# Streaming conv/gated-DeltaNet/PEER layer on one core: a third expert of four is multiplied in rounded pieces, and GpSimd subtracts the first table's remainders

## The reference, cut to what matters

```python
q = (x2 @ w_q).reshape(n, PEER_HEADS, 2, PEER_HALF)
s = jnp.einsum('nhpd,hpkd->nhpk', q, sub_keys)      # top 16 per half, then top 16 of the 256 sums
...
hid = jnp.einsum('pd,phkd->phk', xb, u[ib])         # first table, rows u
act = jax.nn.gelu(hid) * gb                         # gb: softmax gates of the 128 chosen experts
return jnp.einsum('phk,phkd->pd', act, v[ib])       # second table, rows v
```

## Time and profile before

| | |
|---|---|
| median of 3 runs | 4827.29 us (4825.91 to 4842.75) |
| the profiled execution, its own time | 4846.23 us |
| its span | 4844.7 us |
| TensorE busy | 4618.2 us, 95% |
| VectorE, ScalarE, GpSimd busy | 3317.9, 1250.0, 1277.3 us (68%, 26%, 26%) |
| DMA busy from 3,600 us on | 0.97 of 16 engines |

### The profile page before, as it was taken

One profiled execution on the slowest core, in us unless ns is written; L12 is line 12 of the kernel. 1 busy time (PEld: TensorE's weight loads), 2 busy tenths in 40 slices (PEclk: granted clock), 3 DMA queues, 4 the chain that ended last, 5 costly groups with the idle time before them and its releaser, 6 DMA issues. The chain is left out here.

```text
span 4844.7 us, 82402 instructions
## 1 busy us (share of the span) xinstructions
PE 4618.2 (95%) x27693; PEld 4287.9 (89%) x27693; DVE 3317.9 (68%) x4283; ACT 1250.0 (26%) x1766; POOL 1277.3 (26%) x936
## 2 busy tenths in 40 slices
PE   8999989999998999999679999999999999999995
PEld 8999989999997999999668888888888888888884
DVE  4889873343433330168887888888888888888887
ACT  4232323222222221232462222222222222222221
POOL 0111132221122332233002333333333333332332
PEclk8999999999999999999899999999999999999997
DMA  3222223221234342221378999999999999999998
GB/s 117 85 89 85 87 66 97 71 74 55 71 95 158 122 158 89 96 97 60 105 227 336 361 351 365 366 362 368 368 362 369 364 372 362 366 366 367 365 360 326
DMA packets 283622, 1084.63 MB, mean 224 GB/s; under 512 B 23696, under 2 KB 104464, under 8 KB 209936
## 3 DMA queue, kind: packets, MB, share of 16 engines
q0 software_dynamic: 74752, 538.99, 28.8%
q1 hardware_dynamic: 168336, 400.91, 25.1%
q10 hardware_dynamic: 40320, 142.10, 7.6%
HBM read 1017.03 MB, written 64.88 MB: 223 GB/s over the span
## 5 line engine op out<-in xcount | busy, mean ns | idle before, releaser
L486 PE MATMUL ps<-xhi,hi 128*128 128x320 f32 x2560 | 773.5, 315 | 31.2 <-POOL lo L1388 15.8
L486 PE MATMUL ps<-xlo,hi 128*128 128x320 f32 x2560 | 761.7, 311 | 0.0
L2479 PE MATMUL ps<-aT,work 128*128 128x384 f32 x2048 | 750.1, 489 | 4.1 <-DMA work<-in_v_units 4.1
L2445 PE MATMUL ps<-xhi,whi 128*128 128x384 f32 x2048 | 692.1, 338 | 0.0
L2445 PE MATMUL ps<-xlo,whi 128*128 128x384 f32 x2048 | 686.4, 335 | 0.0
L2797 DVE CUSTOM_DVE_ANT_0 work<-work,keep 128x2048 f32<-128x2048 f32 x256 | 585.1, 2286 | 33.4 <-DMA work<-in_peer_u,cur_u 22.1
L2762 DVE SCALAR_TENSOR_TENSOR keep<-work,act_w,keep 128x2048 f32<-128x2048 f32 x256 | 600.5, 2346 | 7.3 <-DMA work<-in_peer_v,cur_v 5.9
L2487 PE MATMUL ps<-ahi,vhi 128*128 128x384 f32 x1024 | 495.1, 484 | 32.2 <-DVE vlo L2735 32.0
L486 PEld LDWEIGHTS ps<-xhi,hi 128*128 128x128 f32 x2560 | 484.8, 189 | 36.3 <-POOL lo L1388 16.3
L2860 POOL DMA_INDIRECT work<-in_peer_v,cur_v x256 | 306.3, 1196 | 797.7 <-DVE keep L2762 770.5
L2479 PEld LDWEIGHTS ps<-aT,work 128*128 128x128 f32 x2048 | 381.6, 190 | 142.7 <-issue 7.7
(11 more groups left out here) (334 smaller groups left out, 7760.5 us busy)
## 6 DMA issues: line engine op xcount, KB each, us to landing
work<-in_v_units ACTq DMA_DIRECT2D x256, 512.0 KB, 8.0
work<-in_u_units SPq DMA_DIRECT2D x240, 512.0 KB, 8.0
keep<-in_w_first SPq DMA_DIRECT2D x160, 512.0 KB, 3.6
keep<-in_w_units SPq DMA_DIRECT2D x32, 1024.0 KB, 4.9
gates_dram<-work SPq DMA_DIRECT2D x8, 3072.0 KB, 11.8
gbuf<-gates_dram SPq DMA_DIRECT2D x31, 768.0 KB, 9.9
arena<-in_w_units SPq DMA_DIRECT2D x32, 512.0 KB, 4.0
gates_T<-keep SPq DMA_DIRECT2D x32, 320.0 KB, 2.2
```

The source lines that it names most:

```text
L486: m = pe.matmul(out[:, o:o + HT], w[:, k, :], x[:, 8 * kh + k, c], start=kh == 0 and i == 0, stop=kh == 1 and i == 23)
L2445: pe.matmul(out, h3[:, k, :], (xlo if m % 2 else xhi)[:, 8 * half + k, :], start=half == 0 and m == 0, stop=False)
L2479: pe.matmul(out, w4[:, q, e, :], aT[:, (1 - par) * WHOLE + e, :], start=e == 0, stop=False)
```

## The change

`SPLIT` goes from 2 to 3, so `WHOLE` from 2 to 1: a third expert of each four has its unrounded product replaced by three rounded ones, with its own rounding and remainder of the weights (`vhi`, `vlo`) and of the activations (`ahi`, `alo`). `vhi` and `vlo` are now made in two pieces, one for each half `q`, each with a count of its own, and TensorE waits for each piece. `vlo` is written over the loaded weights. The first table's remainder `wlo` is made by GpSimd from chunk 2 on, in two pieces of 512 columns a unit, between its two indirect DMAs; VectorE makes it only in chunk 1 and before.

```diff
-SPLIT = 2
+SPLIT = 3
 WHOLE = ET - SPLIT
...
+        vlo = [workr[:, RAW + i * UNIT:RAW + (i + 1) * UNIT].rearrange("p (d e c) -> p d e c", d=2, e=ET)[:, :, WHOLE:, :] for i in (2, 3, 0, 1)]
...
@@ second table on TensorE
                         for e in range(WHOLE):
...
-                            pe.matmul(out, w4[:, q, e, :], aT[:, (1 - par) * WHOLE + e, :], start=e == 0, stop=False)
-                        if q == 0:
-                            wait_count(pe, "pe", vlo_done, c * NU + (j + 1 - NU))
+                            pe.matmul(out, w4[:, q, e, :], (a0 if is_first(c) else aT[1 - par])[:, e, :], start=e == 0, stop=False)
+                        wait_count(pe, "pe", vlo_done, c * (2 * NU) + (2 * j + q + 1 - 2 * NU))
                         for e in range(SPLIT):
...
@@ high_v on ScalarE
-                act.activation(vhi[:, r, :].rearrange("p (d e c) -> p d e c", d=2, e=SPLIT), raw, ACT.Copy).then_inc(vhi_done, 1)
+                for d in range(2):
+                    act.activation(vhi[r][d].rearrange("p (e c) -> p e c", e=SPLIT), raw[:, d], ACT.Copy).then_inc(vhi_done, 1)
...
-                    if j == NU - 1 and has_u:
-                        high_a(c * SPLIT, 0, par * SPLIT)
+                    if j % 2 and j >= 2 * WHOLE + 3 and has_u:
+                        e = (j - 3) // 2
+                        high_a(c * SPLIT + (e - WHOLE), e, par)
...
@@ low_v on VectorE
-                v.tensor_tensor(lo, raw, hi.bitcast(F32), ALU.subtract).then_inc(vlo_done, 1)
+                for d in range(2):
+                    wait_count(v, "dve", vhi_done, n * 2 + (d + 1))
+                    hi = vhi[r][d].rearrange("p (e c) -> p e c", e=SPLIT)
+                    v.tensor_tensor(vlo[slot][:, d], raw[:, d], hi.bitcast(F32), ALU.subtract).then_inc(vlo_done, 1)
...
@@ phase on VectorE
-                    if has_u and not (j == NU - 1 and is_last(c)):
-                        if first and j < NU - 1:
-                            low_pre(NU + j + 1, (NU + j + 1) % PRE, (j + 1) % 2)
-                        else:
-                            low(c * NU + (j + 1), (j + 1) % 2)
+                    if first and j < NU - 1:
+                        low_pre(NU + j + 1, (NU + j + 1) % PRE, (j + 1) % 2)
...
@@ GpSimd
+            def low(n, r):
+
+                wait_count(pool, "pool", hi_done, n + 1)
+                wait_count(pool, "pool", lo_done, n + 2)
+                for i in range(2):
+                    cols = slice(i * UNIT // 2, (i + 1) * UNIT // 2)
+                    ins = pool.tensor_tensor(wlo[:, r, cols], uraw[r][:, cols], whi[:, r, cols].bitcast(F32), ALU.subtract)
+                ins.then_inc(lo_done, 1)
...
                         rows(urow[0 if alone else j % 2], peer_u, cur_u[:, h, w:w + 1], u_ld[j % 2])
+                    if has_u and not first:
+                        low(c * NU + j, j % 2)
+                    if gu:
                         if w == QG - 2 and not (h and last):
```

More of the change, by code:

```diff
@@ L1486, in build @@
         with ExitStack() as later:
-            vlo = later.enter_context(nc.sbuf_tensor("vlo", [P, 2, 2 * SPLIT * P], F32R))
+            alo1 = later.enter_context(nc.sbuf_tensor("alo1", [P, SPLIT, TD], F32R))
         sel = ctx.enter_context(nc.sbuf_tensor("sel", [P, SELW], F32))
@@ L2240, in build @@
         whi, wlo = sb2("whi", [P, 2, UNIT], F32R), sb2("wlo", [P, 2, UNIT], F32R)
+        with ExitStack() as later:
+            later.enter_context(nc.sbuf_tensor("a_gap", [P, WHOLE, TD], F32))
+            a0 = later.enter_context(nc.sbuf_tensor("a0", [P, ET, TD], F32))
         aT = sb2("aT", [P, 2 * WHOLE, TD])
-        ahi, vhi = sb2("ahi", [P, 2 * SPLIT, TD], F32R), sb2("vhi", [P, 2, 2 * SPLIT * P], F32R)
+        ahi_all, vhi0 = sb2("ahi", [P, 2 * SPLIT, TD], F32R), sb2("vhi", [P, 3, SPLIT * P], F32R)
+        aT = [aT[:, (1 - i) * WHOLE:(2 - i) * WHOLE, :] for i in range(2)]
+        ahi = [ahi_all[:, (1 - i) * SPLIT:(2 - i) * SPLIT, :] for i in range(2)]
+        alo = [alo0, alo1]
+        vhi = [[vhi0[:, 0, :], vhi0[:, 1, :]], [vhi0[:, 2, :], vhi1[:]]]
         rows2 = keep[:, 2 * KD * TD:2 * KD * TD + 2 * GT * D]
@@ L2250, in build @@
         gbuf, hbuf = sb2("gbuf", [P, TD // GTOK, ET * GTOK]), sb2("hbuf", [P, 2, TD])
+        with ExitStack() as later:
+            workr = later.enter_context(nc.sbuf_tensor("workr", [P, KD * TD + 4 * D + 4 * UNIT], F32R))
         work = sb2("work", [P, KD * TD + 4 * D + 4 * UNIT])
@@ L2484, in phase @@
                                 wait_count(pe, "pe", a_done, c * ET + (WHOLE + e + 3 - ET))
[L2485 to L2489, removed]
+                            vh = vhi[j % 2][q][:, e * P:(e + 1) * P]
+                            vl = vlo[j % 2 if has_u else j % 4][:, q, e, :]
+                            a_h, a_l = ahi[1 - par][:, e, :], alo[1 - par][:, e, :]
+                            pe.matmul(out, vh, a_h, start=False, stop=False)
+                            pe.matmul(out, vh, a_l, start=False, stop=False)
+                            mmi = pe.matmul(out, vl, a_h, start=False, stop=e == SPLIT - 1)
                         mmi.then_inc(v_mm, 1)
@@ L2672, in times_stage @@
             def times_stage(n):
-                part = aT[:, 0:ET, n * GTOK:(n + 1) * GTOK]
+                part = a0[:, 0:ET, n * GTOK:(n + 1) * GTOK]
                 v.wait_ge(g_evac, (n + 1) * NBB + 2)
@@ L2705, in _ @@
                 v.wait_ge(a_hi, e + 1)
-                v.tensor_tensor(alo[:, e, :], aT[:, WHOLE + e, :], ahi[:, e, :].bitcast(F32), ALU.subtract).then_inc(a_done, 1)
+                v.tensor_tensor(alo[0][:, e, :], a0[:, WHOLE + e, :], ahi[0][:, e, :].bitcast(F32), ALU.subtract).then_inc(a_done, 1)
             v.sem_inc(v_add, 4)
```

47 lines of the change are left out of this document (23 added, 24 removed).

## The result

The changed kernel takes 4929.45 us (median of 4, 4919.51 to 4942.13) against 4835.02 us (4825.91 to 4846.93): ratio 1.019, interval 1.0171 to 1.0209. The prediction was 4789 us with 4850 as its upper end.

What follows compares the result with a forecast made beforehand. TensorE's own instructions were taken as the bound, with DMA close behind. A unit of 8.72 us, 0.16 less, saves 248 x 0.16 = 40 us, less 1 us at chunk starts: 4807 us profiled, 4789 us median; range 4766 to 4850.

Steps and rivals of the forecast that it cites:

- TensorE's part: TensorE's unit: three rounded products replace one unrounded a half, saving 0.12 us, so 8.88 us becomes 8.64 us.
- The ceiling: The most the kernel could gain from TensorE's shorter units: 248 x 0.24 = 59.5 us.
- GpSimd's time: GpSimd's remainder subtractions: 1.3 us a piece of 512 columns, 2.6 us a unit (2.3 to 2.85).
- GpSimd's piece starts beside the sum and hides about 0.65 us. That state has a period of about 9.42 - 0.65 = 8.77 us: Once VectorE is late, GpSimd's subtraction overlaps VectorE's sum out of PSUM by 0.65 us: period about 8.77 us.
- The sum with nothing covered, 9.42 us: VectorE's unit if none of GpSimd's subtractions falls under the PSUM sum or a wait: 6.82 + 2.6 = 9.42 us.
- VectorE and GpSimd bound each other, slower: Rival: GpSimd's pieces hold VectorE at the end of `gather_add`; 4885 us with 0.3 us covered, 4957 with none; chance 0.16.
- behind instructions of VectorE without a gap GpSimd needed 18.79 us ... which would favour VectorE: Which engine gets the shared SBUF ports: two GpSimd subtractions took 18.79 us in an earlier trace, taken to favour VectorE.
- The fetch of `v` rows: GpSimd's row fetch behind the subtractions: comes 3.1 us later, still hidden with 1.6 us left.
- the floor of 8.72 us: DMA engines' time a unit: 8.63 us of packets, at most 99% busy over long stretches, so 8.72 us.
- 40 us: Forecast saving over the units: 0.16 us less a unit, 248 x 0.16 = 40 us.
- some tens: TensorE's waits for `vlo`: forecast to grow from 4.5 us to some tens of us.

Runs made afterwards that it cites:

- the kernel without loops: Experiment 1's kernel with its chunks written out in place of the two loops over pairs of chunks: 4794.57 us, ratio 0.9914 to the kernel before.
- experiment 1: The changed kernel with the first table's remainder made by VectorE again, three rounded products kept: 4826.01 us, ratio 0.9978 to the kernel before.
- loops of four chunks: Experiment 1's kernel with the two loops over pairs of chunks written as loops over four: 4824.69 us, ratio 0.9971 to the kernel before.
- experiment 6: The changed kernel with GpSimd's two subtractions a unit made copies of u's 512 columns, subtraction of whi left out: 4860.56 us, one run.
- Memsets: The changed kernel with GpSimd's two subtractions a unit replaced by memsets of 512 columns, remainder left out: 4838.81 us, one run.

## Why the prediction was wrong, step by step

- **TensorE's part: right.** Without a wait two units of the kernel without loops start at 2873.44 and 2882.04, 8.60 us; 8.64 was predicted, and a half takes 2.21 us (2.22). The ceiling is 248 x 0.28 = 69 us.
- **GpSimd's time: right.** Two pieces take 2.53 us where nothing holds them, 2.8 in the mean (1.40 each); 2.6 was taken, with 2.85 as the upper end.
- **"GpSimd's piece starts beside the sum and hides about 0.65 us. That state has a period of about 9.42 - 0.65 = 8.77 us": the step that failed.** The sum with nothing covered, 9.42 us, was nearly the truth: 220 `gather_add`s in 2,050 us are 9.32 us a unit (loop turn-rounds included). In steady units nearly nothing is covered (added up over the records from 2,650 to 4,700 us, GpSimd's pieces and the sum lie side by side for 0.06 us a unit, where 0.65 was expected), since `gather_add`'s end releases the fetch that stands ahead of the subtraction in GpSimd's queue. The queue's order puts the subtraction one fetch under the dot product and one fetch more behind `gather_add`'s end, and that sum is just VectorE's way to the next `gather_add`. I placed the piece by `whi` alone. `whi` was mostly there earlier: GpSimd waited for it ahead of a subtraction for 54 us in 2,100, in 34 waits.
- **The rival "VectorE and GpSimd bound each other, slower" was right**, with chance 0.16 and 4885 to 4957 us; 4929 is 0.1 to 0.2 us covered. Its place was wrong: I had the first piece ahead of the dot product, and it is inside `gather_add`.
- **"behind instructions of VectorE without a gap GpSimd needed 18.79 us ... which would favour VectorE": misread.** There VectorE had sixteen instructions in 16.82 us and GpSimd lost each time. Here VectorE loses to two subtractions. Which one loses isn't a property of an engine, and a row from another stage couldn't settle it.
- **The fetch of `v` rows: right,** hidden, in spite of an issue of 2.1 us instead of 0.96.
- **DMA: the floor of 8.72 us is none.** In the kernel without loops windows with a DMA share of 0.98 or 0.99 and 377 to 385 GB/s have TensorE full at 8.60 us a unit.
- **A term was missing.** Even with the lock gone 40 us would not have come: experiment 1 gained 10 (19 in the stretch). The prediction took TensorE's waits for "some tens" and priced them at nothing. VectorE's unnamed waits stood in the trace of before (22.3 us in the group of `wlo`) and cost TensorE next to nothing there. I asked neither what they were nor what covered them. About 23 us are the turn-rounds. Some 27 us more are missing from the ceiling of 69; TensorE's waits for late `vlo`s and loads in the kernel without loops are 24.5 us of it (up to 4,700 us).

What stays open: why loops of four chunks returned nothing although VectorE's waits went, how much of the turn-rounds' cost is slack and how much is the second wait, whether two loads in flight would help, and why the copy of experiment 6 and the subtraction differ in who is held. Holding the subtraction back until the sum out of PSUM is under way wasn't tried.

## What to carry to other kernels

Before moving work to GpSimd, add up the VectorE instructions with two SBUF operands and the GpSimd instructions that read SBUF as if they were one engine's; if the sum, with what can't be hidden, passes the period, take it for the new bound (9.42 us by the sum here, 9.32 measured). Assume no overlap unless the order of the queues forces it, and look for it in the mean length of the instructions, not in the waits. And before shortening the unit of the engine that sets the time, list the rare stalls of its suppliers (loop turn-rounds, slow landings): they may cost nothing today and come out when the unit is shorter. Here writing the loops out changed nothing in the old kernel's time and gave experiment 1's kernel 31 us between medians, 23 of them in the stretch.

## What the runs showed of the hardware

- A GpSimd subtraction reading two SBUF operands held a `gather_add` of 2.35 us for its whole 2.53 us (5.04 us in all), both pieces back to back, although the records have `gather_add` starting 0.35 us earlier. Memsets held nothing (2.346 us); copies cost VectorE 0.3 us a unit and took 1.43 us themselves, 0.60 at the shortest. The Trainium skill (SBUF — State Buffer, "SBUF: two separate sides") gives the pair to whoever starts first. By that rule the memsets agree, since it has VectorE contend only with a GpSimd operation that reads; the recorded starts of `gather_add` and the subtraction don't.
- The issue of an indirect DMA on GpSimd took 0.96 us alone and 2.1 to 2.7 us under the dot product.
- At the turn-round of the first loop VectorE stood twice in one turn, 0.97 to 3.75 us each (experiment 1), and TensorE twice, 2.8 and 2.85 us, with no releaser named; without loops these waits are gone from TensorE. An 8 KB packet of the instruction queue starts 1.8 to 2.0 us before VectorE's first record behind each of its waits; in the kernel without loops no unnamed wait of VectorE above 0.6 us has one. The Trainium skill (Runtime: NRT & Kernel Launch, "Instruction fetch mechanics") says that a taken branch to code outside the engine's window must fetch it by DMA first. The runs agree in place, cure and packets.
